# Where low parts of weight blocks are made, and where the early expert rows are summed, in a one-layer decoder kernel

## The reference

```python
def _peer(h, w_query, sub_keys, u_tab, v_tab):
    qry = (h @ w_query).reshape(T, PEER_HEADS, 2, D_KEY_HALF)
    sc = jnp.einsum('thpc,pnc->thpn', qry, sub_keys)
    ...                                  # two top-16, combined, top-16 again: eidx, best_s
    gate = jax.nn.softmax(best_s, axis=-1)
    u = u_tab[ib]
    a = jax.nn.gelu(jnp.einsum('bd,bhkd->bhk', hb, u), approximate=False) * gb
    return jnp.einsum('bhk,bhkd->bd', a, v_tab[ib])
```

## Time and profile before

| | us |
|---|---|
| median of 3 runs | 4683.04 |
| lowest and highest | 4677.85, 4700.03 |
| the profiled execution, own time | 4692.95 |
| its span, first to last instruction | 4690.9 |
| TensorE busy in it | 4582.4 (98%) |
| VectorE, GpSimd, ScalarE busy | 3113.9, 1443.7, 1235.5 |
| gate blocks, first to last gate product | 581.8 |
| rest of the u stage, chunks 63 to 127 | 885.5 |

### The profile page before, as it was taken

The page is one execution under the profiler, slowest core; times in us unless marked ns, Lnnn a source line. Parts: engine busy times, 40 slices in busy tenths (PEclk is TensorE's granted clock), DMA queues, the critical chain, the costliest instruction groups (busy, mean ns, idle before and its releaser), DMA issues.

```text
span 4690.9 us, 83265 instructions
## 1 busy us (share of the span) xinstructions
PE 4582.4 (98%) x33385; PEld 4497.4 (96%) x33385; DVE 3113.9 (66%) x5137; ACT 1235.5 (26%) x1633; POOL 1443.7 (31%) x1036
## 2 busy tenths in 40 slices
PE   8999999999999999999999999999999999999997
PEld 8999999989999999999999999999999999999997
DVE  6643442334425789489999546577748889988844
ACT  4113332133223122221111222112123343332332
POOL 1000000010000014433333344667625447656300
...
GB/s 211 164 167 114 119 149 171 153 154 170 189 138 130 150 171 148 146 183 188 177 163 175 164 223 279 243 324 331 327 216 382 358 346 371 382 353 341 164 81 89
DMA packets 538039, 997.19 MB, mean 213 GB/s; under 512 B 45583, under 2 KB 386079, under 8 KB 503711
## 3 DMA queue, kind: packets, MB, share of 16 engines
...
...
## 4 chain that ended last, share of the span: by engine, by line
PE 72%; DVE 16%; PEld 6%; issue 2%; DMA 2%; POOL 1%; ACT 1%; ACTq 0%; PEldq 0%; SPq 0%; DVEq 0%; POOLq 0%
PE PS L2065 49%; PE PS L2566 19%; PEld PS L2065 6%; DVE oh_i L1752 5%; DVE oh_i L1755 3%; DVE g_st L1728 2%; DVE oh_j L1751 2%; DMA w_raw<-in_w 1%; DVE sum L1866 1%; DVE w_lo L1184 1%; ACT w_hi L781 0%; PE PS L2173 0%; POOL a_y L699 0%; PE PS L2199 0%; DMA v_raw<-in_w 0%
## 5 line engine op out<-in xcount | busy, mean ns | idle before, releaser
L2065 PE MATMUL PS<-h_hi,w_hi 128*128 128x288 f32 x7808 | 2334.4, 299 | 35.6 <-DVE w_lo L1184 22.0
L2065 PE MATMUL PS<-h_lo,w_hi 128*128 128x288 f32 x7808 | 2313.3, 296 | 3.5 <-issue 3.3
L2065 PE MATMUL PS<-h_hi,w_lo 128*128 128x288 f32 x7808 | 2313.4, 296 | 2.2 <-issue 2.1
L2065 PEld LDWEIGHTS PS<-h_hi,w_hi 128*128 128x128 f32 x7808 | 1477.3, 189 | 66.3 <-issue 36.1
L2065 PEld LDWEIGHTS PS<-h_lo,w_hi 128*128 128x128 f32 x7808 | 1477.6, 189 | 5.3 <-issue 4.6
L2065 PEld LDWEIGHTS PS<-h_hi,w_lo 128*128 128x128 f32 x7808 | 1478.2, 189 | 3.8 <-issue 3.8
L781 ACT ACTIVATE w_hi<-w_raw 128x1024 fp32r<-128x1024 f32 x522 | 553.4, 1060 | 2521.9 <-PE PS L2065 2324.3
L1184 DVE TENSOR_TENSOR w_lo<-w_raw,w_hi 128x1024 fp32r<-128x1024 f32 x388 | 478.4, 1233 | 834.4 <-ACT w_hi L781 774.4
L646 POOL TENSOR_TENSOR w_lo<-w_raw,w_hi 128x1024 fp32r<-128x1024 f32 x136 | 342.0, 2514 | 546.6 <-ACT w_hi L781 546.6
L737 POOL DMA_INDIRECT rows<-v_rows,row_i x134 | 204.0, 1522 | 304.8 <-DVE acc L1909 228.4
L729 POOL DMA_INDIRECT a_el<-act_scr,act_i x160 | 262.1, 1638 | 51.3 <-issue 51.3
...
## 6 DMA issues: line engine op xcount, KB each, us to landing
...
v_rows<-in_w ACTq DMA_DIRECT2D x512, 256.0 KB, 3.7
v_raw<-in_w SPq DMA_DIRECT2D x128, 512.0 KB
act_scr<-gsp POOLq DMA_DIRECT2D x128, 288.0 KB
...
```

Of the source, the lines that this page charges most:

```text
L2065: ins = mm(dst[:, a], w[:, m, at + n], xx[:, k, a * TH:(a + 1) * TH], start=first and n == 0 and r == 0, stop=last and n == len(ks) - 1 an ...
```

## The change

Four things are changed.

1. **Low parts in the gate blocks.** `put` on GpSimd no longer makes them in chunks 24 to 62 (78 blocks, two of them at the edges are still GpSimd's). VectorE makes them in `one_hots`, six to a block of the gate, behind the masks of steps 0, 1, 3, 4, 5 and 7 (`SPLIT_AT`). The high parts of the gate values, before made in each block, are made once for all tokens (`g_hi`), so each block has one small copy and one subtraction less, and one copy more.
2. **The sums of the early passes** are kept in PSUM banks 0 to 3 and not in SBUF. At the end of a pass (`SUM_AT`) ScalarE copies the 2048 columns out to one of four buffers, and the next pass waits for that copy.
3. **Row buffers and lead.** There are four row buffers and not six, rows are sent one chunk ahead and not two, and 16 picks of the first pass move by up to one chunk.
4. **The folds** of all four passes stand behind one another after chunk 123.

```diff
-FOLD_AT = [t0 + w + 1 for t0, w in PASS_AT]
+SUM_AT = [t0 + w for t0, w in PASS_AT]
+FOLD_AT = SUM_AT[-1] + 1
...
-NR_Y = 6
+NR_Y = 4
+SPLIT_AT = {0: 0, 1: 1, 3: 2, 4: 3, 5: 4, 7: 5}
...
+        sum_y = [at("sum_0", [P, D], F32, rZ)[:], *(sums_y[:, q] for q in range(3))]
 
         def row_y_buf(i):
-            return rows_x[:, i] if i < 3 else rows_m[:, i - 3]
+            return rows_x[:, i] if i < 1 else rows_m[:, i - 1]
...
                 for c in range(GATE_T):
-                    put(UA + GATE_T * u + c, loops, GATE_T)
+                    put(UA + GATE_T * u + c, loops, GATE_T, False)
+                if u == ND - 1:
+                    pool.wait_ge(s_lo, B_U + 2 * (UA + UG))
+                    split(B_U + 2 * (UA + UG))
...
                 for n in range(NY):
-                    if Y_AT[n] == t + 2:
+                    if Y_AT[n] == t + 1:
                         row_y(n)
...
+                if t in SUM_AT:
+                    p = SUM_AT.index(t)
+                    act.wait_ge(S["axpy"], NR_Y + TY * (p + 1))
+                    nc.scalar.activation(sum_y[p], PS[:, 0:4].rearrange("p b c -> p (b c)"), ACT.Copy
+                                         ).then_inc(S["gx"], 1)
...
                 ch.did(v.tensor_copy(oh_cur[:, u], gij_t[:, bass.ds(at_step(GT * b, [(r, 2 * GT) for r in loops]), GT)]))
-                ch.wait()
-                ch.did(v.tensor_copy(oh_hi[:, u], oh_cur[:, u, :, 0]))
-                ch.wait()
-                ch.did(v.tensor_tensor(oh_cur[:, u, :, 0], oh_cur[:, u, :, 0], oh_hi[:, u].bitcast(F32), ALU.subtract))
+                ch.did(v.tensor_copy(oh_hi[:, u], g_hi[:, bass.ds(at_step(GT * b, [(r, 2 * GT) for r in loops]), GT)]))
...
+                    key = B_U + 2 * (UA + GATE_T * b) + SPLIT_AT.get(n, 0)
+                    if n in SPLIT_AT and (loops or key >= B_U + 2 * UA + 2):
+                        split(key, [(r, 4 * GATE_T) for r in loops])
...
+                acc_y = PS[:, 0:4].rearrange("p b c -> p (b c)")
                 if n % TY:
                     dve.wait_ge(S["axpy"], NR_Y + n)
-                    v.scalar_tensor_tensor(sum_y[p % 2][:], row_y_buf(n % NR_Y), a_y[:, n:n + 1], sum_y[p % 2][:],
-                                           ALU.mult, ALU.add).then_inc(S["axpy"], 1)
+                    v.scalar_tensor_tensor(acc_y, row_y_buf(n % NR_Y), a_y[:, n:n + 1], acc_y, ALU.mult,
+                                           ALU.add).then_inc(S["axpy"], 1)
                 else:
-                    if p >= 2:
-                        dve.wait_ge(S["gx_t"], p - 1)
-                    v.tensor_scalar(sum_y[p % 2][:], row_y_buf(n % NR_Y), a_y[:, n:n + 1], None, ALU.mult
+                    if p:
+                        dve.wait_ge(S["gx"], p)
+                    v.tensor_scalar(acc_y, row_y_buf(n % NR_Y), a_y[:, n:n + 1], None, ALU.mult
                                     ).then_inc(S["axpy"], 1)
...
+            with pe.Fori(0, (FOLD_AT - UA - UG) // 2) as i:
+                for u in range(2):
+                    plain(UA + UG + 1 + u, [i])
             for p in range(NP):
-                if (FOLD_AT[p] + 1 - t) % 2:
-                    plain(t)
-                    t += 1
-                with pe.Fori(0, (FOLD_AT[p] + 1 - t) // 2) as i:
-                    for u in range(2):
-                        plain(t + u, [i])
                 folded(p)
```

37 lines of the change are left out of this document (20 added, 17 removed).

## The result

The changed kernel takes **4718.5 us** (median of 5 runs, 4715.57 to 4722.63) beside 4695.5 for the kernel before (median of 5). The ratio is 1.0057, with a 95% interval of 1.0032 to 1.0081: half a per cent slower, by 15 to 38 us. The forecast was 4665, a little faster. 4718 lies inside the range given (4632 to 4730), but on the other side of no change. A second measurement of the same kernel beside other runs gave 1.0058.

What follows compares the result with a forecast made beforehand. VectorE was taken to bound the gate blocks, its masks held by GpSimd's subtractions, and TensorE the chunks right behind. -35 + 17 + 0 on 4692.95 us gave 4675; the median being 9.9 lower, 4665 us, range 4632 to 4730.

Steps and rivals of the forecast that it cites:

- The 4 us for a low part that comes 0.3 late in each block: Gate blocks: the sixth low part, behind step 7, reaches TensorE 0.3 us late, 13 times: 4 us.
- the floor: Gate blocks: TensorE's least time for a gate step, 36 products and a bundle, 5.25 us; 540.4 for 103 steps.
- the start of the first block: First gate block: first sums and masks are behind anyway, costing another 2 to 3 us, an estimate.
- 10.9 + L: Early passes: way from one gated product to the next, L being a row's landing, 5.0 us: 15.9 against TensorE's 12.7.
- seven pairs at 2.2 and three single ones: Early passes: TensorE's waits, 15.4 us for seven chunk pairs plus 4.1, 1.6 and 0.6 at chunks 90, 99, 112: 21.7.
- the debt: Early passes: each next chunk begins 3.2 us late; in every third chunk `fused` replaces the row and the lateness goes.
- the prediction's own slope: Early passes: each further us of row landing costs one us in each of some 17 chunks.
- The relief of -5: Early passes: sums in PSUM no longer hold GpSimd's picks and row issues, put at -5 us.
- rival B: Chunks 88 to 116: rows land late, sharing DMA engines with loads, gates and fused values; 4700 to 4735 us, chance 0.18.
- ScalarE's copy of the sums, put at 0 and 0.6: Early passes: four copies of 2048 columns stand where ScalarE waits, 0; chunk 112's row waits for one, 0.6 us.
- the same 64 products move: 0: Folds after chunk 123: moving the same products there changes nothing, 0 us.
- The -16 for that stretch: Around chunk 90, ahead of the first fold: end of range if TensorE's loss there of 16 to 20 us goes.

Runs made afterwards that it cites:

- part 1 alone: The kernel before with only the low parts of chunks 24 to 62 moved to VectorE, early passes and folds as before: 4663.2 us, ratio 0.9958.
- the experiment on the ends: Changed kernel with VectorE's wait moved behind the first masks and GpSimd's first low part of chunk 63 ahead of the put: 4704.1 us, ratio 1.0050.
- the three experiments: Changed kernel, rows ahead of picks: 0.9957; changed kernel, rows sent two chunks ahead: 0.9994; kernel before, rows sent one chunk ahead: 1.0115.

## Why the prediction was wrong

**Sign and size.** Forecast: -35 for part 1, +17 for part 2, 0 for part 3, so -18. In the two profiles: -17.5, +21.5 and +20.4. Three folds left the stretch of part 2 for that of part 3, 3 x 3.6 = 10.7 us; put back, part 2 is +32 and part 3 +10. How much of part 2 the slow stretch at chunk 90 hides is not settled: part 1 alone, which lacks that stretch, took 800.3 us where the kernel before took 804.0, since its waits elsewhere were longer (27.3 us against 12.9).

**Part 1, the bound: right.** VectorE was the bound, masks were held by GpSimd, and with the subtractions moved the gate products run in 553 us, 2 above the 541 to 551 that were named. That it is so near is partly luck. The 4 us for a low part that comes 0.3 late in each block are not in the trace (between the two ends the profile has no wait of TensorE in the gate blocks), but a step takes 552.7 / 103 = 5.37 us where the floor had 5.25. **The step that failed** is "the start of the first block ... costs another 2 to 3, an estimate", and that the end had no term at all. They cost 6.3 and 7.7. The `dve.wait_ge` ahead of the first masks was among the edits (it is the line that the experiment on the ends takes away); what had to be asked is what is queued behind it (all masks of the first two steps) and when GpSimd's part that it waits for is done. Likewise the `split` behind `if u == ND - 1` had been moved behind a `put` that waits for the activation. With both mended, part 1 gives 31 us by its profile, close to the 35.

**Part 2, the loop: right, its price too low.** 10.9 + L with L = 5 gave 15.9 us; measured in one turn were 16.8. Order and lead decided, as the three experiments show. **The step that failed** is the sum over chunks: seven pairs at 2.2 and three single ones. It took each wait at its own length and the debt as paid off in every third chunk. The trace has 18 waits in these chunks, 47.8 us in all and 14 of them over 1.1 us, where 21.7 were forecast. One term under that sum was undersized: L was taken at 5.0, the shortest of the three gathers that VectorE waited for before (5.0, 9.8 and 11.6 us), and of the 50 it waited for in the changed kernel the median is 6.8. By the prediction's own slope, one us in each of some 17 chunks, those 1.8 us alone come to 31, an estimate, and would cover the 26 that were missing. Rows behind `gated` wait as well (landing was up to 11.3 us), which the sum left out, and a wait brings the half clock: 25 to 28 us more in chunks 64 to 122. The relief of -5 was undersized too: the PSUM sums are worth 34 us, but next to a loop that the lead had made. The loss had been named (rival B: rows land late in the loop, 4700 to 4735) with 0.18; its place and its price fit the result. Its sign, rows waited for 8 us and more, came once in 50; how much of the loss is its longer landing, and how far full DMA engines made it so, no run separates. A smaller term is ScalarE's copy of the sums, put at 0 and 0.6: VectorE waited 7.5 us for copies ahead of the first rows of passes.

**Part 3: the step that failed** is "the same 64 products move: 0". The same products cost 3.6 us each fold alone and 22.5 in a row. The prediction counted products and not the time of one at either clock, and no row of before had more than one fold at a time. The clock of 0.74 ahead of the first fold was kept apart from the folds, and that holds: the same gaps came in kernels without a fold there. The -16 for that stretch came and went between kernels with the same code; that the changed kernel was without most of it is luck.
